# Modulation pieces and expert chunks in another order, modulation matmuls in column halves

## The reference

```python
# first block
h = h + pool_mixer(rmsnorm(h, a_norm), a_w, a_scale)
h = h + hierarchical_moe(rmsnorm(h, ffn_norm[0]), ...)   # 32 experts, top 2 of one group
k_nope, k_rope, v = shared_latent_kv(h, ...)
h = h + mla_mixer(rmsnorm(h, b_norm), ...)
h = h + hierarchical_moe(rmsnorm(h, ffn_norm[1]), ...)
x = rmsnorm(h, final_norm)[:, N_META:]
# each expert
y = (silu(xb @ w_gate[e]) * (xb @ w_up[e])) @ w_down[e]
# second block, per layer
def ada_mod(c, w, b):
    m = (silu(c) @ w + b)[:, None, :]                    # 1024 x 3072
    shift, scale, gate = split(m, 3)
    return shift, scale, 1.0 + gate
shift, scale, gate = ada_mod(c, ada_w[layer, 0], ada_b[layer, 0])
x = layer_norm(ALPHA * x + gate * mixer(x * (1 + scale) + shift), ...)
shift, scale, gate = ada_mod(c, ada_w[layer, 1], ada_b[layer, 1])
u = x * (1 + scale) + shift
x = layer_norm(ALPHA * x + gate * (square(relu(u @ mlp_w1 + b1)) @ mlp_w2 + b2), ...)
```

## Time and profile before

| what | us |
|---|---|
| median of 3 runs | 2542.47 |
| lowest, highest | 2537.54, 2543.96 |
| the profiled execution | 2534.56 |
| its span | 2532.5 |
| TensorE busy | 2309.3 (91%) |
| VectorE busy | 1246.9 (49%) |
| ScalarE busy | 781.9 (31%) |
| GpSimd busy | 125.7 (5%) |

### The profile page before, as it was taken

One profiled execution on the slowest core, in us unless ns is written; L12 is line 12 of the kernel. 1 busy time (PEld: TensorE's weight loads), 2 busy tenths in 40 slices (PEclk: granted clock), 3 DMA queues, 4 the chain that ended last, 5 costly groups with the idle time before them and its releaser, 6 DMA issues.

```text
span 2532.5 us, 27589 instructions
## 1 busy us (share of the span) xinstructions
PE 2309.3 (91%) x10608; PEld 1586.9 (63%) x10608; DVE 1246.9 (49%) x1906; ACT 781.9 (31%) x1367; POOL 125.7 (5%) x154
## 2 busy tenths in 40 slices
PE   6899997998889999799788999998987888999997
PEld 4533333876744333377567888876666776788886
DVE  5411114556731111578456555558747845633455
ACT  4211113455211111453124232233316642422321
POOL 1111110000001111100000000000000000000000
PEclk9999998999889999899779999999989999999999
DMA  5799996220679998532013443322100031322320
GB/s 204 264 394 401 388 363 234 92 67 1 227 304 399 385 390 335 197 116 94 23 50 108 150 150 127 123 100 84 67 17 1 1 133 67 104 87 100 117 75 34
DMA packets 90850, 416.19 MB, mean 164 GB/s; under 512 B 16600, under 2 KB 16960, under 8 KB 51408
## 3 DMA queue, kind: packets, MB, share of 16 engines
q1 hardware_dynamic: 71024, 373.26, 38.7%
q0 software_dynamic: 19696, 41.17, 4.5%
HBM read 516.34 MB, written 31.98 MB: 217 GB/s over the span
## 4 chain that ended last, share of the span: by engine, by line
PE 74%; DVE 16%; DMA 4%; ACT 3%; issue 2%; SPq 0%; POOL 0%; DVEq 0%; ACTq 0%; POOLq 0%
PE psum L109 15%; PE psum L110 15%; PE psum L111 14%; PE psum L868 13%; PE psum L891 6%; PE psum L1688 2%; DVE w_low L309 2%; PE psum L858 2%; DMA raw_in_x<-in_moe 1%; DMA raw<-in_ada 1%; DVE w_low L1032 1%; DVE ada_sums L1723 1%; ACT w_high L285 1%; DVE gla_head L2361 1%; DMA rows<-in_rows 1%
## 5 line engine op out<-in xcount | busy, mean ns | idle before, releaser
L309 DVE TENSOR_TENSOR w_low<-raw,w_high 128x2048 fp32r<-128x2048 f32 (+2 forms) x110 | 245.5, 2238 | 249.6 <-ACT w_high L285 235.5
L109 PE MATMUL psum<-x_high,w_high 128*128 128x512 f32 x848 | 348.1, 410 | 16.7 <-DVE x_low L1032 9.8
L110 PE MATMUL psum<-x_high,w_low 128*128 128x512 f32 x848 | 339.3, 400 | 0.0
L111 PE MATMUL psum<-x_low,w_high 128*128 128x512 f32 x848 | 337.3, 398 | 0.0
L285 ACT ACTIVATE w_high<-raw 128x2048 fp32r<-128x2048 f32 (+2 forms) x110 | 204.7, 1870 | 297.7 <-PE psum L111 280.5
L111 PE MATMUL psum<-w_low,mlp_high 128*128 128x512 f32 x512 | 202.2, 395 | 0.0
L110 PE MATMUL psum<-w_high,mlp_low 128*128 128x512 f32 x512 | 201.5, 393 | 0.0
L109 PE MATMUL psum<-w_high,mlp_high 128*128 128x512 f32 x512 | 200.5, 392 | 0.9 <-DVE mlp_low L1032 0.9
L109 PEld LDWEIGHTS psum<-x_high,w_high 128*128 128x128 f32 x848 | 160.5, 189 | 64.1 <-ACT u_tile L1818 6.9
L110 PEld LDWEIGHTS psum<-x_high,w_low 128*128 128x128 f32 x848 | 160.2, 189 | 43.8 <-issue 6.3
L111 PEld LDWEIGHTS psum<-x_low,w_high 128*128 128x128 f32 x848 | 160.4, 189 | 39.1 <-issue 0.6
(11 more groups left out here) (552 smaller groups left out, 4120.0 us busy)
## 6 DMA issues: line engine op xcount, KB each, us to landing
raw<-in_moe SPq DMA_DIRECT2D x72, 1024.0 KB
raw_in_x<-in_moe SPq DMA_DIRECT2D x72, 1024.0 KB
raw<-in_mlp SPq DMA_DIRECT2D x64, 1024.0 KB
raw_in_high<-in_moe SPq DMA_DIRECT2D x54, 1024.0 KB
raw_in_low<-in_moe SPq DMA_DIRECT2D x54, 1024.0 KB
raw<-in_ada SPq DMA_DIRECT2D x48, 1024.0 KB
raw_extra<-in_moe SPq DMA_DIRECT2D x36, 1024.0 KB
raw<-in_evin SPq DMA_DIRECT2D x10, 1024.0 KB
```

The source lines that it names most:

```text
L109: pe.matmul(out, ah, bh, start=first, stop=False)
L110: pe.matmul(out, al, bh, start=False, stop=False)
L111: return pe.matmul(out, ah, bl, start=False, stop=last)
L309: dve.tensor_tensor(wl[:, 0:w], k.RAW[k.RAW_AT[c]][:, 0:w], wh[:, 0:w].bitcast(F32), ALU.subtract).then_inc(*k.V.step("low", c))
```

## The change

It has six parts.

- `load_list`: the first eight modulation pieces stood together behind the first chunk. Now three stand there, then come four chunks of experts 0, three pieces, six expert chunks and two pieces. At experts 1 the twelve pieces of step 2 are taken out of the queue behind attout, so the four pieces of step 1 stand alone ahead of the experts' chunks. Behind each of the chunks 3 to 26 of the first MLP stands one piece of step 2 or 3, where behind every second one of 3 to 25 there was one of step 3.
- `place_chunks` gives the freed split-weight slots an age that makes them the first to be taken, and the ones that wait for the end of routing the last.
- `ada_rows` issues two matmuls of 64 stationary columns and 256 moving columns for one of 128 and 512, one for each side of the array. `ada_pick` is one multiply with a table of 64 columns and one reduction.
- Step 2's pieces and sums go from attout and route 1 into the first MLP. All share one accumulator, so the first multiply of an even piece waits for the sums of the piece before.
- In route 1 the groups (1,1) and (1,2) go ahead of the norm turns; their picks go to the end of VectorE's routing. Route 0's group (0,2) goes to another bank.
- TensorE goes into the expert stages unbarred.

```diff
 def load_list(k):
-    follow = {0: late[0:8]}
+    follow = {0: late[0:3], k.MOE0[0] + 3: late[3:6], k.MOE0[0] + 9: late[6:8]}
     follow[k.FIRST[("latent",)] + 1] = late[8:14]
-    follow[k.FIRST[("attout",)] + 3] = [(2, n) for n in range(ADA_PARTS)] + late[14:18]
+    follow[k.FIRST[("attout",)] + 3] = late[14:18]
     follow[k.MOE0[1] + MOE_CHUNKS - 1] = late[18:24]
-    for n in range(ADA_PARTS):
-        follow.setdefault(k.FIRST[("mlp", 1)] + 3 + 2 * n, []).append((3, n))
+    for n in range(2 * ADA_PARTS):
+        follow.setdefault(k.FIRST[("mlp", 1)] + 3 + n, []).append((2 + n // ADA_PARTS, n % ADA_PARTS))
...
-                    raw_age[r], raw_holds[r] = n - 2 + (w_age[w] + SPLIT_SLOTS) / (n + SPLIT_SLOTS + 1), w_holds[w]
+                    raw_age[r], raw_holds[r] = -2 + (w_age[w] + SPLIT_SLOTS) / (n + SPLIT_SLOTS + 1), w_holds[w]
...
 def route_tensor(k, pe, L, T):
+    if L:
+        for g in (1, 2):
+            pe.wait_ge(*k.after("att done", g - 1))
+            ada_rows(k, pe, 1, g, 3 + g, ADA_HALF)
...
-    ada_rows(k, pe, L, 1, 7)
+    if L == 0:
+        ada_rows(k, pe, 0, 1, 7)
...
-        ada_rows(k, pe, 0, 2, 2)
-    if L:
-        for n in range(ADA_PARTS):
-            ada_sums(k, pe, 2, n, 6)
-        pe.wait_ge(*k.after("modulation", 2))
+        ada_rows(k, pe, 0, 2, 7, ADA_HALF)
...
-    if L:
-        pe.wait_ge(*k.after("ada picked", 1, 1))
-        ada_rows(k, pe, 1, 2, 7)
...
 def ada_rows(...)
-            mm = pe.matmul(k.PS[:, bank, :], k.CS[:, f:f + 1].to_broadcast([P, P]), w[:, i * ADA_COLS:(i + 1) * ADA_COLS],
-                           start=(f == 0), stop=(f == DK - 1))
+            moving = w[:, i * ADA_COLS:(i + 1) * ADA_COLS].rearrange("p (a q c) -> p q a c", q=ADA_SIDES, c=ADA_SIDE)
+            for q in range(ADA_SIDES):
+                side = slice(q * ADA_SIDE, (q + 1) * ADA_SIDE)
+                mm = pe.matmul(k.PS[side, bank, at:at + 4 * ADA_SIDE].rearrange("p (a c) -> p a c", a=4),
+                               k.CS[:, f:f + 1].to_broadcast([P, ADA_SIDE]), moving[:, q, :, :], start=(f == 0), stop=(f == DK - 1))
...
 def ada_piece(k, dve, s, n):
-            if s == 3 and n:
-                dve.wait_ge(*k.after("ada sums", s, n - 1))
+            if s == 3 or n:
+                dve.wait_ge(*k.after("ada sums", *((s, n - 1) if n else (2, ADA_PARTS - 1))))
...
 def mlp_pieces(n):
-    return [(3, a) for a in range(ADA_PARTS) if 3 + 2 * a == n]
+    return [(2 + a // ADA_PARTS, a % ADA_PARTS) for a in range(2 * ADA_PARTS) if 3 + a == n]
...
-UNBARRED = [("tensor", "even_in"), ("tensor", "mlp"), ("tensor", "fox_in")]
+UNBARRED = [("tensor", "moe"), ("tensor", "even_in"), ("tensor", "mlp"), ("tensor", "fox_in")]
```

More of the change, by code:

```diff
@@ L484, in pool_vector @@
     V = k.V
+    dve.tensor_reduce(k.SIDE[:, :], const(k, "ident").rearrange("p (q c) -> p c q", q=ADA_SIDES), AX.X, ALU.add).then_inc(*V.step())
     bands_vector(k, dve)
@@ L1638, in attout_vector @@
     c = k.FIRST[("attout",)]
-    split_low(k, dve, c + 1)
-    for n in range(6):
-        ada_piece(k, dve, 2, n)
-        if n in (1, 2):
-            split_low(k, dve, c + n + 1)
+    split_low(k, dve, c + 3)
     for half in range(2):
-        if half:
-            for n in range(6, ADA_PARTS - 2):
-                ada_piece(k, dve, 2, n)
         for t in range(XT):
@@ L1678, in ada_source, with ada_rows @@
     return src[:, 4 * (n % 2):4 * (n % 2) + 4, j * ADA_COLS:(j + 1) * ADA_COLS]
-def ada_rows(k, pe, s, g, bank, pieces=None):
-    for n in pieces or (2 * g, 2 * g + 1):
+def ada_rows(k, pe, s, g, bank, at=0):
+    for n in (2 * g, 2 * g + 1):
         pe.wait_ge(*k.after("raw", (s, n)))
@@ L1687, in ada_rows, with ada_pick @@
             f = 4 * (n % 2) + i
[L1688 to L1689 removed]
+            moving = w[:, i * ADA_COLS:(i + 1) * ADA_COLS].rearrange("p (a q c) -> p q a c", q=ADA_SIDES, c=ADA_SIDE)
[3 more added lines that the diff above has]
+                               k.CS[:, f:f + 1].to_broadcast([P, ADA_SIDE]), moving[:, q, :, :], start=(f == 0), stop=(f == DK - 1))
         mm.then_inc(*k.T.step("raw free", (s, n)))
     k.T.mark("ada rows", s, g)
[L1694 removed]
+def ada_pick(k, dve, s, g, bank, at=0):
     dve.wait_ge(*k.after("ada rows", s, g))
     dve.wait_ge(*k.V.now())
[L1698 to L1702 removed]
+    rows = k.PS[:, bank, at:at + 4 * ADA_SIDE].rearrange("p (a c) -> p a c", a=4)
+    dve.tensor_tensor(rows, rows, k.SIDE[:, :].unsqueeze(1).to_broadcast([P, 4, ADA_SIDE]), ALU.mult).then_inc(*k.V.step())
+    dve.wait_ge(*k.V.now())
+    dve.tensor_reduce(k.MODC[:, s, 4 * g:4 * g + 4], rows, AX.X, ALU.add).then_inc(*k.V.step("ada picked", s, g))
 def ada_total(k, s, n):
[L1707 removed]
+    return k.ACC[:, :]
 def ada_piece(k, dve, s, n):
@@ L1747, in ada_done @@
     else:
-        dve.wait_ge(*k.after("ada sums", s, ADA_PARTS - 1))
-        src = k.PS[:, 6 if s == 2 else 3, 0:3 * DK]
+        dve.wait_ge(*k.after("ada sums", 3, ADA_PARTS - 1))
+        src = k.PS[:, 3, 3 * DK * (s - 2):3 * DK * (s - 1)]
         dve.tensor_copy(k.MODC[:, s, 2 * DK:3 * DK], src[:, 2 * DK:3 * DK]).then_inc(*k.V.step())
@@ L3384, in program @@
     k.SQR1 = k.at("route_squares_late", [P, D], k.XLAT)
-    k.ACC6 = k.at("ada_sums", [P, ADA_PARTS // 2, ADA_COLS], k.end)
     k.GATE = k.at("gate", [P, 2, XT + 1], k.keep)
@@ L3390, in program @@
     k.AID = k.at("assignments", [P, 4 * (XT + 1)], k.end, I32)
+    k.SIDE = k.at("side_ident", [P, ADA_SIDE], k.end)
     k.XG = k.at("xg", [P, XG_SLOTS, D], k.SCR)
```

30 lines of the change are left out of this document (11 added, 19 removed).

## The result

The changed kernel takes 2561.42 us (median of 7 runs, 2551.88 to 2571.28) against 2537.85 (7 runs, 2535.29 to 2545.91): the ratio is 1.0086, 95% interval [1.0059, 1.0113]. It is slower by 0.86%, at the very end of the stated range (2561), where the likeliest case said no change (2543). The ratios of this document compare the levels of all runs and are not quotients of two medians: the 94 measured runs of the kernel before lie in two groups, 35 at 2529 to 2539 us and 59 at 2540 to 2550, so its median moves by several us with the share of each. The profiled execution of the changed kernel took 2561.42 us, and its span is 2559.4, 26.9 us more than before. A table of places in the program, read from both traces, says where they come from.

What follows compares the result with a forecast made beforehand. TensorE, busy 91% of the span, was taken as the bound, with DMA also near its limit in the experts. Gains of -29.5 and losses of +30.4 gave +0.9 us on the median: 2543 us, range 2518 to 2561.

Steps and rivals of the forecast that it cites:

- the start: Up to the first expert product: shorter first modulation groups bring it at 104.0 for 106.84 us, -2.8 (0 to -4).
- rival 3: First MLP: half clock behind each of six gaps costs 18 us for 5, plus experts' give-back; 2560 us, chance 0.13.
- part 4: First MLP: 24 pieces make TensorE wait for mlp_low and mlp_y, +25.4 us, and +5 for low clock.
- The rival of an absorbed cost: First MLP takes the pieces without waiting, only 5.7 us lost; 2519 us, chance 0.27.
- part 2: Expert chunks loaded ahead of pieces: starting stalls go, 1.5 us given back each; experts 0 -10.0, experts 1 -5.2 us.
- rival 4: Experts: stalls turn into a wait a few pairs later, +10 us in both together; 2553 us, chance 0.11.
- The terms for a start at half clock: Experts' first products run at a low clock: +1 us at experts 0, +2.5 at experts 1.
- part 3: Routing 1: sums gone, two groups ahead of norm turns, first expert products at 725.5 for 732.27 us, -6.8 (-3 to -9).
- part 1: Modulation matmuls in two column halves running at once: 3.5 us saved per group, at start, latent and enter.
- rival 2: Modulation groups: the column halves don't run at once, +13.5 us; 2557 us, chance 0.09.
- latent: -3.5: Latent stage: the last modulation group on the chain gets shorter, 3.5 us saved (0 to -4).
- enter: -1.2: Enter stage: a shorter group on the chain saves 1.2 us, limited by x_low's readiness (0 to -3.9).

Runs made afterwards that it cites:

- prefetch_first: Kernel before, with only the new load order of the first experts (ten chunks ahead) and its slot ages: 2531.53 us, ratio 0.9965.
- best_one: Changed kernel, both MLP pieces per quarter moved, first and enter modulation groups in old form, last experts 0 chunks outside plain raw slots: 2518.64 us, ratio 0.9917.
- best_short_start: best_one with the first modulation group in column halves: 2514.97 us, ratio 0.9899 against the kernel before.

## Why the prediction was right and where it was not

**The headline: missed, and held by the range through luck.** The forecast was +0.9 us, the profile has +26.9. The terms that were off are the start (+7.1 for -2.8), latent (+4.4 for -3.5) and enter (+4.6 for -1.2), together 23.6 us; all others together are 2.4 us off. The upper end of the range came from rival 3, whose mechanism (half clock behind each gap of the MLP, 13 us more than the forecast's 5) gave 2.7 more. That the result stands at that end is a coincidence: no rival named what happened at the three places.

**The MLP (part 4): right in place, size and mechanism of the waits.** +25.4 and +5 for the clock were forecast, +31.0 measured. The waits are 3 x 2.95 and 3 x 4.04 us, forecast 2.8 and 3.75 (with 0.95 for the sums, 4.7). The two experiments that move one piece each take out 17.3 and 11.5, together 28.8; with both moved 1.4 us are left. The two smaller terms were mis-sized against one another: of 31.0 us, 20.0 are waits (20.9 less the 0.9 that before had), some 7.7 are low clock, for which 5 were priced, and 3.3 are left for five more sums and the rest, where 5.7 were priced for six. The rival of an absorbed cost had a chance of 0.27 and fell.

**The experts (part 2): mechanism right, give-back too small.** The stalls of 12.5 and 9.2 us at the start went (113.90 to 145.54 is 31.6 us, as without a stall), but one later period is 3.7 and 4.4 us too long, where 1.5 was taken each time. That is rival 4's mechanism, with 5.1 us more in both together where it said 10. The terms for a start at half clock made up for part of it: at experts 0 the priced 1 us didn't come, at experts 1 about 2 of the priced 2.5 did (5.42 for 3.43 us). That both stages came out within 1.2 us of the forecast is in part luck.

**Routing 1 (part 3): right** (-5.9 for -6.8), step by step: groups 7.06 us, turns without a gap, logits 17.9 us after the attention output for 17.9, first product 42.9 after it for 42.1.

**Column halves (part 1): the factor two was right, the gain was not.** At full clock the groups take 3.5 to 3.7 us, and the halves run at once, so rival 2 falls. But the step "latent: -3.5" took the time of a group on the chain as gain and left out what the change does to the queue there. The load order of experts 0 changed the slots of the last expert chunks, the six pieces waited for the end of experts 0 and ran into the store and the reload. The stretch became 4.4 us longer, and is 5.9 us shorter again when the slots are mended; prefetch_first has the same loss with whole groups. The halves alone gain 0.2 us there: the three groups are 1.5 to 3.5 us shorter each, and TensorE's waits for VectorE's xn grow from 13.8 to 20.5 us in all. The step "enter: -1.2" failed in the same way: a faster group frees its slots earlier, and the transfers behind it meet the store, 5.7 us for 2.1, and the reload. That was shown by putting back the old form there alone (-4.8).

**The start: right in most executions, wrong in some.** -2.8 was forecast; the profiles show -2.0 to -4.2 in five kernels with the short group, and +7.1 and +8.7 in two, by half clock during the pooling. The prediction priced half clock at the experts and in the MLP and not at the start, where a group 4.1 us shorter leaves TensorE a gap of 1.9 us and more ahead of some 15 us of small matmuls. That half clock loses the time is shown by the rows; that the gap brings it on is not shown, and what decides between the two outcomes stays open.

**Two cited rules.** By the Trainium skill (TensorE: Matmul & The Clock Gate, Part 1) the half clock is the default and activity releases it. The prediction read that as a fall behind each of the MLP's six waits; the trace agrees for four of the six, and has clock 1.00 from 1394 to 1404 us, around the first wait for mlp_low. The Trainium skill (TensorEngine Tiling (Array Packing), Instruction Overhead) gives each matmul a fixed cost. By it a group was to be some tenths of a us longer than half; 3.67 for 6.95 to 7.1 us is 0.1 to 0.2 over half, so the trace agrees in direction.

**The median and the chances.** The forecast added its difference to a median whose runs lie in two groups; its profile is of the faster one. The change removes the wait ahead of routing 1's turns, adds three behind it and a gap at the start. The runs spread over 19 us in the changed kernel, 7 in best_one and 17 in best_short_start. How much of the ratio comes from this stays open: each kernel has one profile, and the others of its runs show a mean clock only. One sum of the prediction is wrong: two thirds of rivals 2 to 4 (0.33) plus 0.04 is 0.26 and not 0.28.

## What to carry to other kernels

Work that is moved behind a busy engine's back has room by the average and not by the order: look for what stands behind each moved piece in the row of the engine that does it, and put it behind what the bound engine waits for next. When a step gets faster or its buffers change hands, follow the transfers that its buffers release, and ask what small, late-bound transfer they will meet; the chunk that is early in one place is a collision in another. And look at idle time for what runs behind it at a lower clock, at every place where the change makes one.

## What the runs showed of the hardware

- The store of the last expert rows takes 2.1 us when the DMA share is 0.03, and 5.2 to 6.2 us beside 1 MB weight transfers (share 0.99 at latent in the changed kernel). The reload at latent takes 8.3 to 9.1 and 10.5 to 11.4 us.
- Two fp32 matmuls on 64 columns each (128x256 moved) run at once: 32 records in 3.67 us, 16 of 128x512 in 6.95 to 7.1.
- Ten matmuls without a use (20 records of 128x256, 6.27 us), put where TensorE had waited 5.92 us, made the kernel before 0.21% faster (interval 0.04 to 0.38%), though the work behind them came 2.8 us later in the profile.
- The same program up to there, with a gap of 1.9 to 2.5 us ahead of it, ran its pooling at clock 1.00 over 30 to 40 us in one execution and 0.50 in another (first expert product at 102.6 to 104.1 us in three profiles, 113.9 and 115.6 in two). TensorE was busy 10.00 of 10 us in both windows.
